# Hybrid GLA/Fourier step: tokens loaded transposed and normed in place, modulation made as columns, gate row moved late into pass 3, rank product shared

## The reference

```
ada = silu(cond) @ w_ada + b_ada                  # (3 * 1024,) for c and for c_ctx
shift, scale, gate = split(ada, 3)
h = rmsnorm(x, norm_g) * (1 + scale) + shift      # per token: x * rsqrt(mean(x*x) + eps)
z = h @ w_in                                      # q, k, v, gate_a, r_f, r_b, u, gate_b, mg_a, mg_b
g_f, g_b = log_sigmoid(r @ w_alpha + b_alpha) / 16    # r_f, r_b have 16 channels each
...                                               # gated linear attention, Fourier branch, merge
y = rmsnorm(x + gate * (merged @ w_out), final_norm_g)
```

## Time and profile before

| | before |
|---|---|
| median of 3 runs | 1965.89 us (1965.18 to 1968.84) |
| profiled execution | 1968.57 us |
| its span, first to last instruction | 1966.8 us |
| TensorE busy | 1926.9 us (98%) |
| VectorE busy | 1010.6 us (51%) |
| ScalarE busy | 886.7 us (45%) |
| POOL busy | 574.2 us (29%) |
| mean granted TensorE clock | 0.996 |

### The profile page before, as it was taken

One profiled execution on the slowest core, in us unless ns is written; L12 is line 12 of the kernel. 1 busy time (PEld: TensorE's weight loads), 2 busy tenths in 40 slices (PEclk: granted clock), 3 DMA queues, 4 the chain that ended last, 5 costly groups with the idle time before them and its releaser, 6 DMA issues.

```text
span 1966.8 us, 30215 instructions
## 1 busy us (share of the span) xinstructions
PE 1926.9 (98%) x10589; PEld 1775.1 (90%) x10589; DVE 1010.6 (51%) x1873; ACT 886.7 (45%) x1908; POOL 574.2 (29%) x646
## 2 busy tenths in 40 slices
PE   7999999999999999999999998999999999999998
PEld 2899999999999999999999996888888888898886
DVE  3878877684444433544444525666665322333333
ACT  3555667853455455444455225777732011112222
POOL 0236644143333412344333000002830033331122
PEclk9999999999999999999999999999999999999999
DMA  8577878877788778777888868656438666564433
GB/s 325 196 273 274 288 277 320 306 257 243 258 277 276 254 289 280 240 231 265 270 277 280 310 225 324 241 210 252 172 135 270 220 219 211 193 218 149 142 128 128
DMA packets 167327, 476.90 MB, mean 242 GB/s; under 512 B 14546, under 2 KB 53900, under 8 KB 158608
## 3 DMA queue, kind: packets, MB, share of 16 engines
q1 hardware_dynamic: 153360, 424.70, 63.2%
q10 hardware_dynamic: 13824, 50.34, 6.4%
HBM read 310.34 MB, written 155.20 MB: 237 GB/s over the span
## 4 chain that ended last, share of the span: by engine, by line
PE 78%; DMA 3%; POOL 2%; DVE 1%; ACT 1%; issue 1%; SPq 0%; DVEq 0%; ACTq 0%
PE bank L2116 39%; PE bank L2418 10%; PE bank L2370 10%; PE bank L2383 5%; PE bank L2247 3%; PE bank L2214 3%; PE bank L2225 2%; PE bank L2312 2%; PE bank L2236 1%; DMA x_st<-in_x 1%; POOL h_lo L997 1%; DMA qd<-qk_dec 1%; PE bank L2255 1%; PE bank L2297 1%; DMA v_ld<-v_dram 1%; PE bank L2141 1%
## 5 line engine op out<-in xcount | busy, mean ns | idle before, releaser
L2116 PE MATMUL bank<-h_hi,w_op 128*128 128x384 f32 x4032 | 1052.6, 336 | 6.0 <-DVE u L1619 3.0
L2116 PEld LDWEIGHTS bank<-h_hi,w_op 128*128 128x128 f32 x4032 | 729.9, 188 | 9.6 <-issue 9.6
L2116 PE MATMUL bank<-h_lo,w_op 128*128 128x384 f32 x2016 | 673.6, 334 | 0.0
L2116 PEld LDWEIGHTS bank<-h_lo,w_op 128*128 128x128 f32 x2016 | 378.7, 188 | 0.0
L1564 DVE TENSOR_TENSOR w_op<-w_raw,w_op 128x512 fp32r<-128x512 f32 x240 | 185.9, 776 | 110.3 <-ACT w_op L1172 106.7
L1172 ACT ACTIVATE w_op<-w_raw 128x512 fp32r<-128x512 f32 x240 | 150.2, 627 | 164.2 <-PE bank L2116 157.1
L1022 POOL TENSOR_TENSOR decs<-decs,qk_s 128x192 f32<-128x192 f32 x192 | 121.8, 671 | 334.8 <-ACT decs L1246 334.5
L2418 PE MATMUL bank<-in_a,pwa 128*128 128x512 f32 (+1 forms) x960 | 197.3, 368 | 0.0
L2418 PEld LDWEIGHTS bank<-in_a,pwa 128*128 128x128 f32 x960 | 167.3, 189 | 30.0
L2370 PE MATMUL bank<-ow,me_hi 128*128 128x512 f32 x576 | 177.4, 389 | 0.0
L1619 DVE TENSOR_TENSOR outs<-bank,u 128x384 f32<-128x384 f32 x180 | 99.6, 553 | 109.6 <-PE bank L2116 108.4
(11 more groups left out here) (240 smaller groups left out, 2655.4 us busy)
## 6 DMA issues: line engine op xcount, KB each, us to landing
w_op<-wt_dram SPq DMA_DIRECT2D x192, 512.0 KB, 5.5
wt_dram<-w_op ACTq DMA_DIRECT2D x96, 512.0 KB, 4.7
w_raw<-in_w_in SPq DMA_DIRECT2D x48, 768.0 KB, 5.9
w_raw<-in_w_in SPq DMA_DIRECT2D x24, 1024.0 KB, 6.8
qk_dec<-decs SPq DMA_DIRECT2D x48, 384.0 KB, 6.8
mg_dram<-outs SPq DMA_DIRECT2D x24, 768.0 KB, 6.9
swap<-qk_s SPq DMA_DIRECT2D x48, 192.0 KB, 5.8
v_dram<-outs SPq DMA_DIRECT2D x24, 384.0 KB, 4.9
```

Of the source, the lines that this page charges most:

```text
L2116: ins = pe.matmul(bnk, w_op[slot][:, part, k, :], h[:, j, k, :], start=(first and k == 0 and part == 0 and h is h_hi), stop=(k == HK - 1 a ...
```

## The change

- **Tokens.** The host side lays the tokens out transposed as well (`xt`: pass, channel in tile, half, tile, token), and SP loads them straight into `h32`. TensorE turns no tokens any more. ScalarE squares them (`squares`, 768 elements each, into `sq`), the eight channel tiles are added up (`fold_squares`, VectorE at the start, POOL for passes 2 and 3), and one float32 matmul with a matrix of ones (`square_sum`) gives each token's sum of squares on all partitions. ScalarE makes exp(-0.5 ln(mean + eps)) (`root`), VectorE scales (`scale_tokens`), and ScalarE and VectorE modulate (`modulate`), all in place in `h32`.
- **Modulation.** `w_mod` holds the shift and scale columns in 128x128 tiles, in four chunks of 2 MB; chunks 0 and 1 are those of channel tiles 0 to 3. `columns` multiplies each tile as the stationary operand with the two columns of `silc`, which gives columns at once. `modulation` runs once per half of the channels. Two sums of squares stand inside this stream.
- **POOL at the start.** The weight sums of windows 0 and 1, and `a21`, are made on POOL instead of VectorE.
- **Rank product.** The part that both rank products share is made once; ScalarE copies it to `soft`, VectorE adds it (`rank_sum`), and TensorE goes on with product (4, 1) in the same bank.
- **Gate row.** Both halves are loaded in window 18 of pass 3, 32 terms are summed on VectorE from (19, 4) to (22, 6), gathered in window 22 and stored in window 23. The loads that follow the store in SP's list (`kk0`, `w4`, `chan`, the states) stand in window 23 too.

```diff
+X_LOAD = 18
+X_SQUARED = ((19, 4), (20, 4))
+X_SUMMED = ((20, 3), (21, 2))
+X_SCALED = (((20, 6), (21, 0), (21, 1), (21, 2)), ((21, 4), (21, 5), (21, 6), (22, 0)))
+X_MODULATED = (((21, 3), (21, 4), (21, 5), (21, 6)), ((22, 1), (22, 1), (22, 2), (22, 2)))
+SUM_WINDOW = 22
...
         @block.tensor
-            for n in range(4):
-                ada_row(bank[6 + n % 2], wada[n], s_big[n]).then_inc(s_ada, 1)
-            for e in range(3):
-                turn_x0(e)
...
+            def columns(c, a, z):
+                j, half = c % 2, c // 2
+                for t in range(a, z):
+                    at = 2 * (KT * j + HK * half + t)
+                    for k in range(KT):
+                        ins = pe.matmul(bank[6 + half][:, at:at + 2], wmod[c][:, t, k, :], silc[:, :, k], start=k == 0, stop=k == KT - 1)
+                return ins
...
+            def square_sum(out, i):
+                pe.wait_ge(s_fold, 3 * i + 3)
+                return pe.matmul(out[:, 0:BW], ones, sq[:, 0, :], start=True, stop=True)
...
         @block.gpsimd
+            for which in range(3):
+                sum_weights(0, which)
+            pool.wait_ge(s_s, 2)
+            sum_parts(h32[:, 1, 0:HK, :], h32[:, 1, 0:HK, :], h32[:, 0, 0:HK, :], ALU.subtract)
+            for which in range(3):
+                sum_weights(1, which)
...
         @block.vector
+            def scale_tokens(p, e, q):
+                b = x_half(e) if p else e
+                dve.wait_ge(s_xr, 2 * p + e + 1)
+                x = h32[:, b, 2 * q:2 * q + 2, :]
+                dve.tensor_tensor(x, x, rsb[:, b, :].unsqueeze(1).to_broadcast([P, 2, BW]), ALU.mult).then_inc(s_xn, 1)
```

More of the change, by code:

```diff
@@ new lines, in modulate @@
+            def modulate(p, b, q):
+                for k in (2 * q, 2 * q + 1):
+                    for s, a, z in x_sets(p, b):
+                        ins = modulated(h32[:, b, k, a:z], h32[:, b, k, a:z], s, k)
+                ins.then_inc(s_ha, 1)
+            act.preload_act_table_set("natural_log_exp_and_others")
+            for e in range(2):
+                for q in range(4):
+                    squares(0, e, q)
+                act.wait_ge(s_ms, 2 * e + 1)
+                root(0, e, bank[4 + e][:, 0:BW], s_ms, 2 * e + 2)
@@ L1292, in _ @@
+            high_weights(0, 0)
+            high_input(0, 0)
+            act.wait_ge(s_mod, 4)
+            for q in (2, 3):
+                modulate(0, 0, q)
+            for j in range(1, NPROD):
+                high_weights(0, j)
+                if j == 3:
+                    high_input(0, 1)
+                    high_input(0, 2)
+            high_input(0, 3)
+            high_input(0, 4)
             for j in range(NPROD):
@@ new lines, in _ @@
+            for q in range(2):
+                modulate(0, 0, q)
+            fold_squares(1)
+            low_weights(0, 0)
+            low_input(0, 0)
+            for q in range(4):
+                scale_tokens(0, 1, q)
+            for q in range(2):
+                modulate(0, 1, q)
+            modulation(1)
+            for q in (2, 3):
+                modulate(0, 1, q)
+            dve.wait_ge(s_hv, 6)
+            dve.tensor_tensor(s1[:, :, :], h32[:, 1, 0:HK, :], h32[:, 1, HK:KT, :], ALU.add).then_inc(s_s, 1)
@@ new lines, in _ @@
+            for c in range(2):
+                pe.wait_ge(s_big[c], 16)
+                ins = columns(c, 0, 4)
+            ins.then_inc(s_ada, 1)
+            pe.wait_ge(s_big[2], 16)
+            columns(2, 0, 1)
+            square_sum(bank[4], 0).then_inc(s_ms, 1)
+            columns(2, 1, 4)
+            pe.wait_ge(s_big[3], 16)
+            columns(3, 0, 1)
+            pe.wait_ge(s_ms, 2)
+            square_sum(bank[5], 1).then_inc(s_ms, 1)
+            columns(3, 1, 2)
+            pe.wait_ge(s_end3, 16)
```

507 lines of the change are left out of this document (242 added, 265 removed).

## The result

The changed kernel is slower: 1995.86 us (1993.67 to 1996.38, four runs) against 1967.17 us for the kernel before beside it, a ratio of 1.0142 with a 95% interval of 1.0127 to 1.0157. The forecast was 1987 with a range of 1970 to 1996: the median lies 0.14 us inside its upper end, and one of the four runs (1996.38) lies outside. The profiled execution took 1995.97 us with a span of 1994.2, which is 27.4 over the span of before; the forecast for that difference was 21.4.

A forecast was written before the change was run, and what follows sets the result against it. The prediction took TensorE, busy 98% of the span, as the bound. Start +26.5, stream -9.1 and pass 1 waits +4 gave +21.4 us: 1988.2 on the profiled span, 1987 for the median, range 1970 to 1996.

The forecast's parts named there:

- The start: From kernel start to window 1: window 1 begins at 111.1 us instead of 84.6, +26.5 us.
- half speed for all of them: 256 x 0.22: Modulation columns at the start: all 256 two-column TensorE records run at half clock, 0.22 us each, 56.3 us.
- wait before product 1: At the start: TensorE finishes product 0 at 74.3 us and waits 10.2 us, starting product 1 at 84.5.
- POOL beside VectorE: At the start: POOL's two-input work, 8.4 us together, stretches VectorE's two-input instructions to about one POOL instruction's length.
- Three waits (1.8, 1.8 and 1.2) cost 4.8 here: Before product 1: VectorE, held three times by POOL's work, finishes at 84.5 us instead of 79.7.
- In the stream: TensorE's passes: transposes -10.6, sums of squares +2.6, shared rank product -2.8, gate row +1.7, together -9.1 us.
- Bounds 0 and 8 ... I take +4: Windows 20 to 22 of pass 1: new TensorE waits for the fold or late adds, 0 to 8 us, taken as +4.
- In pass 2 ... I take 0: Pass 2: no new wait, since VectorE has 6.6 us less work per window.
- Rival D: Pass 1's new wait at its bound, also in pass 2 or pass 3's gate terms: +29.4, 1995 us; chance 0.11.
- SP's loads and the gate row: SP's token loads in passes 1 and 2 cost 0; gate row store and loads behind it 0, at worst +2 us.
- pass 3's gate terms: Pass 3: 32 gate terms on VectorE, some 0.7 us each against 2.1 us per slot, covered without a wait.

The follow-up runs named there:

- e1: Changed kernel with four float32 matmuls of 512 columns, result unused, ahead of the first modulation column: 1991.55 us, 1.0128 to the kernel before.
- e2: Changed kernel with one float32 matmul of 512 columns, result unused, before each of the 16 column tiles: 2017.56 us, 1.0255 to the kernel before.
- e6: Changed kernel with the modulation made in rows again (`silc` stationary, 512 columns of `w_mod` moving), VectorE's list changed with it: 1980.85 us, 1.0070 to the kernel before.
- e3: Changed kernel with POOL's start-up sums waiting until VectorE has made the low part of product 1's input: 1995.04 us, 1.0140 to the kernel before.
- e9: Kernel of e5 with POOL's sums of window 1 put ahead of `a21` in its list: 1987.33 us, 1.0101 to the kernel before.
- e5: Changed kernel with the seven high and low weights of window 0 made while TensorE is at its columns: 1994.36 us, 1.0138 to the kernel before.
- e7: Changed kernel with the folds of the squares of passes 1 and 2 on VectorE instead of POOL: 1985.39 us, 1.0097 to the kernel before.
- e8: Changed kernel without folds: ScalarE writes squares as fp32r, TensorE adds the eight channel tiles, for all six sums: 1988.31 us, 1.0108 to the kernel before.
- e4: Changed kernel with the second sum of squares of passes 1 and 2 two slots later in window 21: 1997.11 us, 1.0153 to the kernel before.
- e11: Changed kernel with modulation rows, squares added on TensorE, early weights, POOL's first two window 1 sums ahead of `a21`, split token loads: 1966.06 us, 0.9997 to the kernel before.
- e12: Kernel of e11 with POOL's start-up work on VectorE again and low weights of products 1 to 3 back behind s2: 1963.36 us, 0.9976 to the kernel before.

## Why the prediction was right, and where it was off

The direction, the order of the terms and the cause of the largest one were right. That the time fell inside the range is partly luck: it did so by 0.14 us. On the spans, 21.4 forecast became 27.4: the start took 2.3 us less, the waits and the low clock in the passes 6.6 more, the part behind the passes 1.0 more, and 0.7 is left over.

**The start.** Forecast +26.5, measured +24.2. The step "half speed for all of them: 256 x 0.22" measured 256 x 0.213, 1.7 us less. e1 and e2 show the half speed, e6 its price. First product 68.75 against 70.4, second sum of squares 57.23 against 58.6, wait before product 1 9.75 against 10.2, product 1 82.69 against 84.5. The Trainium skill's rule that I had weighed (TensorE: Matmul & The Clock Gate, section LDWEIGHTS: the load's time is its column count over 1.2, with no clock in it) does not hold here: e1 has both pitches for the same instruction in one stretch, 0.113 and 0.213.

**POOL beside VectorE.** The mechanism was right and e3 shows it (7.8 to 3.6 us). Its price was not. "Three waits (1.8, 1.8 and 1.2) cost 4.8 here" counted the hold up to product 1 alone; e3 takes just that away and gains nothing, e9 moves POOL's four sums of window 1 out and gains 7 over e5. So the hold has to be counted over all of VectorE's work beside POOL's list, which ends at 91 us (4.4 of e9's 6.5 us at window 1), and TensorE's low clock behind its stops comes on top. The Trainium skill (SBUF — State Buffer, section SBUF: two separate sides) describes an exclusive lock between VectorE work with two SBUF inputs and GpSimd work, held for a whole instruction; the 2.1 to 2.35 us of VectorE's 0.68 us instructions beside POOL's fold agree.

**In the stream.** -9.1 by durations, and no run here measures its parts (transposes, rank, gate row) one by one. The difference of 3.2 us behind window 1 nearly adds up with it: -9.1, +9.0 waits (13.6 against 4.6), +1.6 of low clock behind the longest, and +1.0 behind the passes (`v_ld` 5.9 against 4.8, but a wait of 1.4 for `qd` is gone, and small ones of 1.2 are new). That makes +2.5; 0.7 is left over.

**The step that failed** is "Bounds 0 and 8 ... I take +4" together with "In pass 2 ... I take 0". Measured: pass 1 waits 7.6 us against 0.8 and loses 1.6 of clock, +8.4 and just over its bound; pass 2 waits 2.7 for the second fold. For pass 2 I had argued from VectorE's half-empty windows, but that wait hangs on the length of POOL's own list from ScalarE's squares on (8.2 us there, 7.8 in pass 1, where I had 6.3), which a free VectorE does not shorten much. e7 and e8, which both take the fold off POOL, have no such wait in pass 2. e4 shows that the slot was not the cause. The clock after a stop was in none of my terms. Rival D (1995) was nearest in number: its mechanism, the bound reached in pass 1 and waits in pass 2, is what the trace shows; waits at the gate terms of pass 3, which it also had, did not come.

**Right by rows:** SP's loads and the gate row cost at most the 1.1 us at `v_ld` (0 to +2); pass 3's gate terms made no wait.

## What to carry to other kernels

Price a job that is moved to POOL by what it does to VectorE's list beside it, over the whole length of POOL's list, and not by VectorE's time saved: here four folds of 3.3 us on VectorE replaced four of 7.3 to 8.2 us on POOL, and the time fell by some 9 us (6.6 on the spans). Where a matrix-vector product can be made with the matrix moving in 512 columns, a form with a new stationary for every two columns is to be priced at half clock, even in a stream without a gap; whether the two columns or the new stationaries do it was not taken apart. A stop of TensorE can cost more than its length: behind the waits of 3.47 us here and 3.50 in e7 the clock fell to 0.50, behind those of 2.70 (at 795.71) and 1.87 (at 444.00) it stayed at 1.00. Shifting a wait to a later slot changes nothing while the engine behind it is late for the same reason.

## What the runs showed that was not expected

- The profile's granted clock reads 1.00 from 11 to 90 us in the changed kernel, while the records are at half speed up to about 87 (columns 0.213 apart, products 0.96 per three records). In e1, where the clock had been raised first, the same columns read 0.50. The column seems to miss the state in which a program starts, until the clock has changed; there the pitch of the records is the safer reading. A window of the changed kernel:

```profile
82.00:86.00 4.00, 3.31 (x10) 3.34 (x11) 4.00 (x3) 0.14 (x1) 4.00 (x2) 1.00 0.54 212
```

My forecast allowed for this in a bracket only.
- VectorE's one-input modulations are held by POOL too: 3.62 us for four in e11, with POOL's weight sums beside them, against 1.65 in e12 without.
- In e2 the mix ran at full speed for some 4 us at 60 us and at half speed before and behind it; the runs do not show why.
- fp32r squares added up on TensorE served the norm in place of a float32 fold, at 1.55 us for eight records at full speed (passes of e8) and 2.91 at half speed (its start).
